# Side matmuls of a two-part transformer block gathered into longer runs on TensorE

## The reference

```
# first block, layer 1 (scan): 8 groups of 8 heads, state 128, head width 64
cb     = C_g @ B_g.T                                  # 256 x 256, one per group
decay  = exp(segsum(dt * a))                          # 256 x 256, one per head
y_diag = (cb * decay, lower triangle) @ (x * dt)      # one per head
out    = rms_group((y_diag + d * x) * silu(z)) @ w_out
# first block, layer 2: latent attention over the 64 best keys of each query
# second block, layer 1 (gated MLP with token mixing), 16 mixing groups of 256 channels
v      = rms_norm(gelu(x @ w_v)); mixed = tril(w_s[g]) @ v[chunk, group] + b_s[g]
out    = (gelu(x @ w_u) * mixed * silu(x @ w_z)) @ w_out
# second block, layer 2 (stick breaking attention), 16 heads of width 128
z      = q @ k.T;  tail = cumulative sum of log_sigmoid(-z) over later keys
a      = exp(log_sigmoid(z) + tail), strictly causal;  o = a @ v
out    = (o * silu(zg)) @ w_out
```

## Time and profile before

| | |
|---|---|
| median of three runs | 2430.32 us |
| profiled execution | 2429.53 us |
| its span | 2428.3 us |
| TensorE busy | 2417.4 us, 19626 records |
| VectorE busy | 1572.8 us |
| ScalarE busy | 1243.5 us |
| memory traffic | 188 GB/s over the span |

### The profile page before, as it was taken

How to read it: one execution, slowest core, us unless ns; L and a number is a source line. 1 busy time by engine, 2 the same in 40 slices (tenths; PEclk the granted TensorE clock), 3 DMA queues, 4 the chain that set the end, 5 groups by cost and what they waited for, 6 DMA issues and landing times.

```text
span 2428.3 us, 45481 instructions
## 1 busy us (share of the span) xinstructions
PE 2417.4 (100%) x19626; PEld 2340.7 (96%) x19626; DVE 1572.8 (65%) x2109; ACT 1243.5 (51%) x1426; POOL 88.4 (4%) x68
## 2 busy tenths in 40 slices
PE   9999999999999999999999999999999999999998
PEld 9999999999999999999988899999999999999998
DVE  6778888866577766665575556656654555555556
ACT  5446665554454565554464445445444446455463
POOL 0001000100031000000000000000000000000002
PEclk9999999999999999999999999999999999999999
DMA  8666656557755655547767666666655576555645
GB/s 248 195 197 183 215 182 186 182 189 244 227 173 164 192 165 152 158 151 244 222 195 237 196 198 192 189 185 193 184 189 187 190 234 208 183 174 174 190 158 182
DMA packets 267434, 467.93 MB, mean 193 GB/s; under 512 B 18955, under 2 KB 70497, under 8 KB 265313
## 3 DMA queue, kind: packets, MB, share of 16 engines
q1 hardware_dynamic: 267233, 465.02, 62.0%
HBM read 452.18 MB, written 4.26 MB: 188 GB/s over the span
## 4 chain that ended last, share of the span: by engine, by line
PE 97%; DVE 1%; ACT 0%; DMA 0%; issue 0%; SPq 0%; ACTq 0%
PE G L703 91%; PE M L703 5%; PE M L716 1%; DMA RAW<-in_ssd_w_in 0%; DMA WS<-in_a_w_s 0%; DVE W1m L1547 0%; DVE W L1547 0%; DVE TT L2268 0%; DVE W2m L1547 0%; DVE W0m L1547 0%; DVE E L1640 0%; ACT W L1126 0%; ACT W0m L1126 0%; DVE RES L2263 0%; DVE E L1681 0%
## 5 line engine op out<-in xcount | busy, mean ns | idle before, releaser
L703 PE MATMUL G<-AA,W 128*128 128x256 f32 x7908 | 939.0, 277 | 1.1 <-DVE W L1547 1.0
L703 PEld LDWEIGHTS G<-AA,W 128*128 128x128 f32 x7908 | 915.7, 188 | 5.7 <-issue 2.7
L1547 DVE TENSOR_TENSOR W<-RAW,W 128x1024 fp32r<-128x1024 f32 x446 | 556.8, 1251 | 365.6 <-ACT W L1126 364.4
L1126 ACT CAST W<-RAW 128x1024 fp32r<-128x1024 f32 x446 | 464.9, 1047 | 463.2 <-PE G L703 454.0
L703 PE MATMUL G<-AA,WY 128*128 128x256 f32 x2508 | 304.3, 277 | 0.0
L703 PEld LDWEIGHTS G<-AA,WY 128*128 128x128 f32 x2508 | 293.0, 188 | 1.7 <-issue 1.4
L1547 DVE TENSOR_TENSOR WY<-RAW,WY 128x1024 fp32r<-128x1024 f32 (+1 forms) x112 | 142.2, 1272 | 74.1 <-ACT WY L1126 74.1
L703 PE MATMUL G<-W0m,YY 128*128 128x256 f32 x1512 | 183.7, 276 | 0.4 <-DVE W0m L1547 0.2
L703 PE MATMUL G<-W1m,YY 128*128 128x256 f32 x1512 | 183.1, 276 | 0.3 <-DVE W1m L1547 0.2
L703 PE MATMUL G<-W,YY 128*128 128x512 f32 x792 | 181.3, 389 | 0.0
L703 PE MATMUL G<-W2m,YY 128*128 128x256 f32 x1488 | 180.4, 276 | 0.0
(11 more groups left out here) (306 smaller groups left out, 2397.3 us busy)
## 6 DMA issues: line engine op xcount, KB each, us to landing
RAW<-in_a_w_in SPq DMA_DIRECT2D x192, 512.0 KB, 3.9
RAW<-in_ssd_w_in SPq DMA_DIRECT2D x160, 512.0 KB, 4.4
RAW<-in_b_w_in SPq DMA_DIRECT2D x128, 512.0 KB, 4.1
RAW<-in_dsa_w_in SPq DMA_DIRECT2D x72, 512.0 KB, 3.7
RAW<-in_ssd_w_out SPq DMA_DIRECT2D x64, 512.0 KB, 4.6
RAW<-in_dsa_w_out SPq DMA_DIRECT2D x64, 512.0 KB, 4.2
RAW<-in_a_w_out SPq DMA_DIRECT2D x64, 512.0 KB, 3.8
RAW<-in_b_w_out SPq DMA_DIRECT2D x32, 512.0 KB, 3.8
```

The lines of the kernel that those rows point to most:

```text
L703: return e.matmul(o, l, r, start=start, stop=stop, skip_group_check=True)
L1126: e.copy(wh[:, 0:n], RAW[:, v % NR, 0:n]).then_inc(*up(cast_done, "cast", v))
L1547: e.tensor_tensor(wl[:, 0:n], RAW[:, v % NR, 0:n], wh[:, 0:n].bitcast(F), ALU.subtract).then_inc(*up(rest_done, "rest", v))
```

## The change

Five edits, in the programs of TensorE and VectorE:

- scan, TensorE: scores and both sets of transposes in one run at turn 10; all eight heads' products in one run at turn 16, behind one wait for the second E x CB;
- scan, VectorE: CB is read at turn 10 behind the first decays, YT is made at turns 16 (two), 17 and 18;
- mixing: the four pairs of products in one run at turn 2, in two PSUM banks in place of four;
- stick: no turn between the output products of the first pair and the scores of the second, on TensorE alone.

```
--- before.py
+++ after.py
@@ -835,7 +835,7 @@
 
         def ssd(g):
             XG = XGB[:, g % 2]
-            for _ in range(7):
+            for _ in range(10):
                 yield
             b = take("cb", g)
             if g == 0:
@@ -843,9 +843,6 @@
                     e.wait_ge(*on("bc", i))
             mm(M[:, b, 0:256], BT[:, g, 0:P], CT[:, g, :], True, True)
             mm(M[:, b, 256:384], BT[:, g, P:T], CT[:, g, P:T], False, True).then_inc(*up(pe_made, "cb_m", g))
-            yield
-            yield
-            yield
             for t in range(2):
                 b = take("xd", g, t)
                 if t == 0:
@@ -853,15 +850,13 @@
                 for f in range(4):
                     last = transpose(M[:, b, f * P:(f + 1) * P], XG[:, f, t * P:(t + 1) * P], ident[:, :])
                 last.then_inc(*up(pe_made, "xd_t", g, t))
-                yield
-            yield
-            yield
-            yield
+            for _ in range(6):
+                yield
             for i in range(2):
                 b = take("ty", g, i)
                 if i == 0:
                     e.wait_ge(*on("read", "xd", g, 1))
-                e.wait_ge(*on("em", g, i))
+                    e.wait_ge(*on("em", g, 1))
                 for q in (2 * i, 2 * i + 1):
                     for r in range(2):
                         h = 2 * q + r
@@ -1004,16 +998,18 @@
         def ev_u5(j):
             yield
             yield
-            for f in range(4):
-                b = take("mx", j, f)
-                if f == 0:
+            for q in range(2):
+                b = take("mx", j, q)
+                if q == 0:
                     e.wait_ge(*on("wr", j))
-                c = 4 * j + f
-                for n in range(2):
-                    last = mm(M[:, b, n * P:(n + 1) * P], V5[:, n, c * P:(c + 1) * P], WR[:, n, f // 2, :],
-                              n == 0, True)
-                last.then_inc(*up(pe_made, "mx_m", j, f))
-                yield
+                for f in (2 * q, 2 * q + 1):
+                    c = 4 * j + f
+                    for n in range(2):
+                        o = f % 2 * T + n * P
+                        last = mm(M[:, b, o:o + P], V5[:, n, c * P:(c + 1) * P], WR[:, n, q, :],
+                                  f % 2 == 0 and n == 0, True)
+                last.then_inc(*up(pe_made, "mx_m", j, q))
+            yield
 
         def set6():
             here(unit_done, "end5", "unit")
@@ -1082,7 +1078,8 @@
                     mm(M[:, b, 0:T], V7[:, 0, h * P:(h + 1) * P], LSB[:, c, 0:T], True, False)
                     mm(M[:, b, P:T], V7[:, 1, h * P:(h + 1) * P], LSB[:, c, T:384], False, True).then_inc(
                         *up(pe_made, "so_m", j, h))
-                yield
+                if p:
+                    yield
 
         def set8():
             here(unit_done, "end7", "unit")
@@ -1650,8 +1647,12 @@
                 e.wait_ge(*on("y_m", g - 2, 3))
                 e.wait_ge(*on("mixed_in", g - 2, 3))
             yield from conv(b, 4 * g, XG, g_of(b))
-            yield
-            yield
+            for _ in range(5):
+                yield
+            e.wait_ge(*on("cs", g))
+            if g > 0:
+                e.wait_ge(*on("y_m", g - 1, 3))
+            decay(g, 0)
             yield
             e.wait_ge(*on("cb_m", g))
             if g > 0:
@@ -1660,13 +1661,6 @@
                 e.wait_ge(*on("triu"))
             e.tensor_tensor(CB[:, :], M[:, bank.get(("cb", g), 0), 0:384], triu[:, :], ALU.mult).then_inc(
                 *up(dve_made, "read", "cb", g))
-            yield
-            yield
-            e.wait_ge(*on("cs", g))
-            if g > 0:
-                e.wait_ge(*on("y_m", g - 1, 3))
-            decay(g, 0)
-            yield
             for t in range(2):
                 bd = dtT[:, t, 8 * g:8 * g + 8].unsqueeze(2).to_broadcast([P, 8, 64])
                 e.wait_ge(*on("xd_t", g, t))
@@ -1698,7 +1693,8 @@
                                        op0=ALU.mult, op1=ALU.add).then_inc(*up(dve_made, "mixed_in", g, q))
                 if q % 2:
                     here(dve_made, "read", "ty", g, q // 2)
-                yield
+                if q:
+                    yield
 
         def gate_z(g):
             for _ in range((15, 13)[g > 0]):
@@ -2067,7 +2063,7 @@
             if j == 0:
                 e.wait_ge(*on("vr"))
             else:
-                e.wait_ge(*on("mx_m", j - 1, 3))
+                e.wait_ge(*on("mx_m", j - 1, 1))
             for n in range(2):
                 e.tensor_scalar(WR[:, n], WM[:, :, :], VR[:, n:n + 1], None, ALU.mult).then_inc(
                     *up(dve_made, "wr", j))
@@ -2083,16 +2079,18 @@
             yield
             for f in range(4):
                 c = 4 * j + f
-                m3 = M[:, bank.get(("mx", j, f), 0), 0:T].rearrange("p (n t) -> p n t", n=2)
-                e.wait_ge(*on("mx_m", j, f))
+                m3 = M[:, bank.get(("mx", j, f // 2), 0), f % 2 * T:(f % 2 + 1) * T].rearrange(
+                    "p (n t) -> p n t", n=2)
+                e.wait_ge(*on("mx_m", j, f // 2))
                 if f == 0:
                     e.wait_ge(*on("bs", j))
                     if j > 0:
                         e.wait_ge(*on("o3_in", j - 1))
                 e.scalar_tensor_tensor(out=Z5[:, f, :].rearrange("p (n t) -> p n t", n=2), in0=m3,
                                        scalar=vc("vg", c), in1=brc(BS[:, f // 2, :], 2), op0=ALU.mult,
-                                       op1=ALU.add).then_inc(*up(dve_made, "read", "mx", j, f))
-                here(dve_made, "mixed", j, f)
+                                       op1=ALU.add).then_inc(*up(dve_made, "mixed", j, f))
+                if f % 2:
+                    here(dve_made, "read", "mx", j, f // 2)
                 yield
             e.wait_ge(*on("mixed", j, 3))
             e.wait_ge(*on("u5", j))
```

More of the change, by code:

```diff
@@ L1662, in ssd @@
                 *up(dve_made, "read", "cb", g))
[L1663 to L1669, removed]
             for t in range(2):
```

## The result

The changed kernel took 2439.22 us (median of six runs, 2437.25 to 2441.44) against 2430.39 us for the kernel before in the same rounds: a ratio of 1.0035, 95% interval 1.0023 to 1.0046. It is 8.8 us slower; 12.7 us had been forecast. The profiled execution took 2437.25 us with a span of 2436.0 us, 7.7 us more than before.

The account below looks back on a forecast made before the run. TensorE, which never waits, was taken to bound the kernel. Scan 10.1 plus sticks 5.0 less 2.4 us saved made it 12.7 us slower, 2443.0 us; own range 2438.6 to 2446.2, final range 2436 to 2448 us.

Parts of the forecast that it names:

- The scan's term: Scan: TensorE waits for the second E x CB in six of eight groups, 8.4 us in all.
- The cover of W0m: Eighth scan group: the first half run no longer covers the wait for remainder W0m, 1.7 us.
- The stick's term: Stick: SPL wanted a unit sooner, TensorE waits 1.26 us in each of four blocks, 5.0 us.
- The saving: TensorE's joined runs: 2.1 us from E,XD half runs, 0.3 us from 44 full-tile switches, 2.4 us together.
- The range: Whole kernel: the forecast's own range, 8.3 to 15.9 us slower, 2438.6 to 2446.2 us.
- only the sticks wait: Rival: the scan's chain moves up enough, only the stick waits remain, +2.6 us, 2433 us; chance 0.08.
- the spreading of waits: Rival: late results delay further units, 0.5 to 1 us more in each of eight groups, 2448 us; chance 0.12.
- The clock kept its upper level: Rival on TensorE's clock: it falls for one unit per group after eight transposes, +22 us, 2465 us; chance 0.01.
- joining is all that happens: Rival: VectorE's results are ready at the new places, 2.4 us saved, 2428 us; chance 0.04.

Follow-up runs that it names:

- the kernel with both places put back and CSB sooner: Changed kernel with scan's joined run at turn 17, stick pairs apart, CSB fetched four turns sooner: 2425.61 us, 4.3 us less than before.
- the cut into quarters: Kernel before with each half run of E,XD cut in two, four runs of 8 records: 2436.21 us, 5.9 us more.
- the kernel with the stick turn back: Changed kernel with the turn between the stick pairs put back on TensorE: 2432.99 us, 3.1 us above before.

## Why the prediction was right, and where its size was off

**Joined runs bring new waits, which outweigh the saving.** Right in kind and in place: E x CB, SPL in four blocks, W0m in the eighth group. From starts, the waits cost 5.2 us in the second to fifth groups, 2.0 in the sixth, 0.4 in the first and seventh together, 1.8 for W0m and 5.0 for SPL: 14.4 us, against 15.1 forecast. The single waits for E x CB were not all in the 1 to 1.8 us that the prediction named: the second to fifth were 1.29 us each, the sixth 1.97, the seventh only 0.24, and the first group, forecast without one, had 0.19.

**The scan's term, 8.4 us for E x CB.** It measured 7.6. In the second group the decays start at 202.06 where they started at 202.57, behind a reciprocal at the same 195.4, and the product is ready at 222.74 for 223.24: VectorE's chain gained all of the 0.49 us that CB gave up, where I had taken 0.13 because of CSB. Against this, the run starts 0.14 us behind the product and not 0.06. Of the groups that wait, CSB was waited for only in the sixth (0.6 us), where the wait of TensorE is the longest, and in the first (0.4 us). The cover of W0m, 1.7 us, measured 1.8.

**The stick's term, 5.0 us.** Measured 5.0, in the profile and in the run with that edit alone.

**The saving, 2.4 us.** This is the term that was mis-sized: it measured 5.8 us (the 14.4 us of waits less the 8.8 us by which the kernel is slower leave 5.6). Without waits, a scan group takes 48.62 us where it took 49.15. So it is in the kernel with both places put back and CSB sooner,

```profile
223.83 2.87 PE L703 MATMUL M<-E,XD 128*64 128x256 f32 x32
...
272.45 2.87 PE L703 MATMUL M<-E,XD 128*64 128x256 f32 x32
```

and the changed kernel's own groups, less their wait, take 48.59. The eight groups save 4.2 us and not 2.3, mixing saves 1.5 us and not 0.2, the sticks 0.04 us a block.

Two things were mis-priced. First, I took the chain's 2.76 to 2.78 us per unit as an undisturbed pace. It is not: a unit that no run precedes takes 2.72 us, as between 509.27 and 511.99 in the eighth group. The 0.04 to 0.06 us over it belong to the run ahead of the unit, and the 44 joins of full-tile runs saved 2.2 us in all where I had 0.3. Second, at that pace a half run of E,XD costs 1.75 us, and the joined run, counted in the same way, 3.05: the join saves 0.45 us in each group, 3.6 us in all where I had 2.1. Of the 0.45 the cut into quarters gives 0.33 as the price of one more run. The other 0.12 lies inside the longer run, and no run shows why.

**The range.** Measured 8.8 us stands near the lower end of the forecast's own range (8.3 to 15.9), and there is luck in that. The lower end was made of smaller waits, with 0.6 us for W0m that has no working, and a saving of at most 3 us. The waits came as forecast, and the saving was nearly twice those 3 us. That slower was forecast, and for these waits, owes nothing to it.

**The Trainium skill's rule** ("TensorE: Matmul & The Clock Gate", "Part 2: What happens when you issue a matmul") that a drain overlaps the next fill, by which joining would save nothing, is further from the runs than my price was: joining saved 5.8 us in all, and in mixing, where all tiles are full, 1.5.

**The rivals.** That only the sticks wait fell, by the list of waits. So did the spreading of waits: no unit behind a held run waited for a remainder. The clock kept its upper level (a granted clock of 0.999 over the span, the level of 2.4 GHz), with 12 records of scores and transposes in one run. That joining is all that happens came true only where the waits were taken away by later places and earlier data: then it made the kernel 4.3 and 6.3 us faster.

## What to carry to other kernels

Where one engine is never idle, as TensorE here, joining its side runs is worth the price of their ends. That price is read from the whole period of a stage, not from the run's own records. But a joined run stands where its last operand is ready, not where its first was: before moving it, compare for each operand the time at which it lay ready with the new place, and move the run later rather than sooner. Then look at what the old runs had covered, and at transfers that had just been in time.

## What the runs showed of the hardware that was not expected

- The main matmuls behind a side run start about 118 ns apart for the first ten or so and 113 ns apart after that, in the scan, the mixing, the sticks and the output projections of the kernel before. It makes 0.04 to 0.06 us for each run.
- One more run of float32 matmuls with 64-column tiles costs 0.33 us (halves cut into quarters), and joining two halves saves 0.45. For runs of full tiles it is 0.04 to 0.06 us.
- The fetch of CSB (1 MB) took 7.1 to 10.1 us to land in different groups and runs, and 6.2 to 8.9 us where it was issued four turns sooner. This spread moved TensorE by up to 1.2 us a group once nothing was left between its landing and the run that needs it (in the kernel with the stick turn back, one group has 2.7 us from the last main matmul to the run, against 1.5 in its neighbours).
